# Experts two at a time on raw f32 weights, in the expert stage of a hybrid decoder layer

## The reference

```python
def hier_moe(h, ...):                       # h: (256, 1024)
    ...
    gates = jnp.sum(one_hot(e_idx, N_EXPERTS) * wts[..., None], axis=1)
    def expert(acc, prm):                   # 32 experts
        wg, wu, wd, gt = prm                # (1024,512), (1024,512), (512,1024), (256,)
        hid = jax.nn.silu(h @ wg) * (h @ wu)
        return acc + gt[:, None] * (hid @ wd), None
```

## Time and profile before

| | |
|---|---|
| Median of three runs | 739.86 us |
| Profiled execution: span, as its page gives it | 794.1 us |
| TensorE, VectorE, ScalarE busy | 771.8, 647.9, 524.6 us |
| Granted TensorE clock, mean | 0.851 |
| DMA | 249.20 MB, mean 314 GB/s |
| First gather, first gate matmul | 209.06, 212.16 us |
| Last matmuls of the scatter start | 783.99 us |

### The profile page before, as it was taken

One profiled execution on the slowest core, in us unless ns is written; L12 is line 12 of the kernel. 1 busy time (PEld: TensorE's weight loads), 2 busy tenths in 40 slices (PEclk: granted clock), 3 DMA queues, 4 the chain that ended last, 5 costly groups with the idle time before them and its releaser, 6 DMA issues.

```text
span 794.1 us, 13163 instructions
## 1 busy us (share of the span) xinstructions
PE 771.8 (97%) x4865; PEld 590.9 (74%) x4865; DVE 647.9 (82%) x579; ACT 524.6 (66%) x577; POOL 139.2 (18%) x190
## 2 busy tenths in 40 slices
PE   6999999999799999999999999999999999999994
PEld 6774774535688888888888888888888888888873
DVE  3631759656869999999899999999899999999895
ACT  4011333544577888787887888787887888787883
POOL 5400200130231122111111122111111122111000
PEclk9988888888788888888888888888888888888887
DMA  9998966943598999999999999999999999999901
GB/s 320 352 369 319 386 241 253 360 170 118 188 321 307 357 359 352 343 355 349 358 343 355 372 343 359 335 358 359 355 335 363 349 359 352 342 358 357 323 1 56
DMA packets 102153, 249.20 MB, mean 314 GB/s; under 512 B 5265, under 2 KB 5325, under 8 KB 100077
## 3 DMA queue, kind: packets, MB, share of 16 engines
q1 hardware_dynamic: 99648, 244.33, 84.9%
q0 software_dynamic: 1008, 3.31, 1.2%
q10 hardware_dynamic: 1470, 1.22, 0.5%
HBM read 247.78 MB, written 1.07 MB: 313 GB/s over the span
## 4 chain that ended last, share of the span: by engine, by line
PE 95%; DVE 2%; DMA 1%; ACT 1%; issue 0%; SPq 0%; DVEq 0%
PE PS L1558 48%; PE PS L1546 8%; PE PS L1507 6%; PE PS L1252 4%; PE PS L1296 4%; PE PS L1525 4%; PE PS L1516 4%; PE PS L1413 3%; PE PS L1308 2%; PE PS L1290 2%; DMA W<-in_w_ada_dram 1%; PE PS L1180 1%; PE PS L1451 1%; PE PS L1325 1%; PE PS L1205 1%; PE PS L1337 1%
## 5 line engine op out<-in xcount | busy, mean ns | idle before, releaser
L1092 DVE TENSOR_TENSOR WL<-W,WH 128x2048 fp32r<-128x2048 f32 x185 | 417.8, 2298 | 36.1 <-ACT WH L711 36.1
L711 ACT CAST WH<-W 128x2048 fp32r<-128x2048 f32 x185 | 346.4, 1907 | 0.0
L1558 PE MATMUL PS<-WH,XT 128*128 128x512 f32 x512 | 152.3, 422 | 1.4 <-DVE XT L1111 1.4
L1558 PE MATMUL PS<-WL,XT 128*128 128x512 f32 x508 | 148.5, 417 | 0.0
L1558 PEld LDWEIGHTS PS<-WL,XT 128*128 128x128 f32 x508 | 97.5, 192 | 30.0
L1558 PEld LDWEIGHTS PS<-WH,XT 128*128 128x128 f32 x512 | 96.7, 195 | 26.6 <-DVE XT L1111 1.5
L458 POOL COPY cur<-PG 128x2 f32 (+1 forms) x31 | 5.7, 184 | 410.0 <-PE PS L1536 409.6
L1558 PE MATMUL PS<-WH,HT 128*128 128x512 f32 x248 | 72.6, 417 | 0.5 <-issue 0.5
L1558 PE MATMUL PS<-WL,HT 128*128 128x512 f32 x248 | 72.5, 417 | 0.0
L1558 PEld LDWEIGHTS PS<-WH,HT 128*128 128x128 f32 x248 | 47.3, 191 | 15.2 <-issue 0.6
L1558 PEld LDWEIGHTS PS<-WL,HT 128*128 128x128 f32 x248 | 47.9, 193 | 14.4
(11 more groups left out here) (242 smaller groups left out, 922.7 us busy)
## 6 DMA issues: line engine op xcount, KB each, us to landing
W<-in_w_gate_dram SPq DMA_DIRECT2D x64, 1024.0 KB, 8.1
W<-in_w_down_dram SPq DMA_DIRECT2D x64, 1024.0 KB, 5.7
W<-in_w_up_dram SPq DMA_DIRECT2D x63, 1024.0 KB, 9.0
W<-in_w_ada_dram SPq DMA_DIRECT2D x16, 1024.0 KB, 7.8
W<-in_w_in_dram SPq DMA_DIRECT2D x12, 1024.0 KB, 7.5
W<-in_w_ada_dram SPq DMA_DIRECT2D x16, 512.0 KB, 5.3
W<-in_w_out_dram SPq DMA_DIRECT2D x4, 1024.0 KB, 7.3
toe<-line_dram POOLq DMA_DIRECT2D x1, 1536.0 KB, 10.7
```

Of the source, the lines that this page charges most:

```text
L711: nc.scalar.copy(WH[(UPE * odd + u) % SPLITS][:], source).then_inc(hi_ready, 1)
L1092: nc.vector.tensor_tensor(low, source, WH[(UPE * odd + u) % SPLITS][:].bitcast(f32), ALU.subtract).then_inc(lo_ready, 1)
L1558: last = nc.tensor.matmul(PS[:, bank, :], lhsT, w[:, q * 512:(q + 1) * 512], start=begin, stop=end)
```

## The change

The expert stage takes two experts, 2i and 2i+1, in each of 16 turns, with 128 token slots, 64 of each. Weights are no longer split: TensorE multiplies them as f32. The array is used as two halves of 64 columns: the even expert's tokens are stationary in columns 0 to 63 and give PSUM rows 0 to 63, the odd one's in the other half, and their matmuls alternate (L1541, L1556, L1571). A turn has 24 such pairs in place of 96 matmuls of split operands. One gather (48 matmuls of 128 columns), one prepare, one scatter and two turnings (with the plain identity, 128 columns) serve both experts. XT, SG and HT are plain f32; HID, WH, WL, HnL and stack2 go. ScalarE copies the first half of XT, VectorE the second.

A unit's rows are now read as `(h p k) f`: a partition gets four (w_down: two) neighbouring rows of the matrix, 8 KB in one piece. H3 is therefore read with a step of 4 columns and GU with a step of 2. The ring has 12 slots as before, a unit of the even and one of the odd expert after each other, and each waits for its own counter, even_used or odd_used. Units 8 to 11 of the first turn go to four extra buffers V, and their ring slots are filled with turn 1's.

The core of the diff:

```diff
-            WL.append(sb(f"WL{slot}", [P, UW], f32r))
+        W = [sb(f"W{slot}", [P, UW]) for slot in range(RING)]
+        V = [sb(f"V{n}", [P, UW]) for n in range(len(SPARES))]      # SPARES = (8, 9, 10, 11)
...
             if u < 4:
-                v = w.rearrange("l e (h k p) f -> h (l e) p k f", p=P, h=2)[u % 2]
+                v = w.rearrange("l e (h p k) f -> h (l e) p (k f)", p=P, h=2)[u % 2]
...
+                    if p == 0 and v in SPARES:
+                        sp.wait_ge(pt_mm, PAIRS)
+                        if v > SPARES[1]:
+                            sp.wait_ge(pv_mm, PAIRS)
+                            sp.wait_ge(gained, 2)
+                        fetch(v, v % 2, V[SPARES.index(v)], spare_in[v])
+                        continue
...
-                    nc.scalar.copy(WH[(UPE * odd + u) % SPLITS][:], source).then_inc(hi_ready, 1)
-                    nc.vector.tensor_tensor(low, source,
-                                            WH[(UPE * odd + u) % SPLITS][:].bitcast(f32), ALU.subtract).then_inc(lo_ready, 1)
-                    nc.vector.tensor_tensor(XT[:, :, 1, :], PS[:, 2, :].rearrange("p (k s) -> p k s", k=DC),
-                                            XT[:, :, 0, :].bitcast(f32), ALU.subtract).then_inc(xt_ready, 1)
+                    nc.vector.tensor_copy(XT[:, 4:8, :], PS[:, 3, :].rearrange("p (k s) -> p k s", k=4)).then_inc(xt_dve, 1)
...
                     for k in range(DC):
+                        first = k // 4 * FF + k % 4
                         for t in range(TT):
                             for part in range(3):
-                                last = nc.tensor.matmul(PS[:, 2, k * SLOTS:(k + 1) * SLOTS], H3[:, part, t, k * P:(k + 1) * P],
-                                                        OH[:, buf, t, 0:SLOTS], start=(t == 0 and part == 0),
+                                last = nc.tensor.matmul(PS[:, 2 + k // 4, k % 4 * P:(k % 4 + 1) * P], H3[:, part, t, first:first + FF - 3:4],
+                                                        OH[:, buf, t, :], start=(t == 0 and part == 0),
                                                         stop=(t == TT - 1 and part == 2))
...
+                def gate_up(n, i, odd):
+                    late = not (turn_in_pass(i, odd) or p)
+                    pe.wait_ge(xt_act, n + 1)
+                    if not late:
+                        pe.wait_ge(scatT_ready, n * 3 + 3)
+                    for u in range(4):
+                        if u == 1:
+                            pe.wait_ge(xt_dve, n + 1)
+                        if u == 3:
+                            transpose_gate(n)
...
+                        for which in (0, 1):
+                            unit_arrived(pe, i, odd, unit_of(u, which), p)
                         for q in range(4):
-                            bank, lhsT, begin, end = outs(q, high)
-                            last = nc.tensor.matmul(PS[:, bank, :], lhsT, w[:, q * 512:(q + 1) * 512],
-                                                    start=begin, stop=end)
-                    last.then_inc(split_used, 1)
+                            k = 4 * (u % 2) + q
+                            for which in (0, 1):
+                                rows = halves_of(which)
+                                last = nc.tensor.matmul(PS[rows, u // 2, :], XT[:, k, rows],
+                                                        unit_at(i, odd, unit_of(u, which), p)[:, q * FF:(q + 1) * FF],
+                                                        start=(k == 0), stop=(k == DC - 1))
+                                if q == 3:
+                                    last.then_inc(unit_used[which], 1)
```

More of the change, by code:

```diff
@@ L101, in sem @@
             return ctx.enter_context(nc.semaphore(name))
[L104 to L107, removed]
-            WL.append(sb(f"WL{slot}", [P, UW], f32r))
+        W = [sb(f"W{slot}", [P, UW]) for slot in range(RING)]
         X = sb("X", [P, TT, D])
-        with nc.sbuf_tensor("Hn", [P, TT, D], f32) as h:
-            Hn = h
-        HnL = sb("HnL", [P, UW], f32r)
+        Hn = sb("Hn", [P, TT, D])
         G2 = sb("G2", [P, D])
@@ L376, in _ @@
+                with sp.Fori(2 if p == 0 else 1, TURNS) as i:
+                    for v in range(UPT):
+                        sp.wait_ge(unit_used[v % 2], i * UPE + (first + v // 2 + 1 - UPE))
+                        fetch(v, i * 2 + v % 2, W[slot_of(BASE + v)], unit_in[slot_of(BASE + v)])
             stream(0)
@@ L1509, in gather, with turn_over_half @@
                                                         stop=(t == TT - 1 and part == 2))
-                    last.then_inc(gather_mm, 1)
+                        if k % 4 == 3:
+                            last.then_inc(gather_mm, 1)
+                def turn_over_half(up, done):
+                    for k in range(FC):
+                        first = up * FF + k // 2 * 2 * P + k % 2
+                        last = nc.tensor.matmul(PS[:, up, k * P:(k + 1) * P], GU[:, first:first + 2 * P - 1:2], ident[:],
+                                                start=True, stop=True)
+                    last.then_inc(done, 1)
@@ L1524, in transpose_up, with prepare @@
-                    for q in range(FC, 2 * FC):
-                        last = nc.tensor.matmul(PS[:, 0, q * SLOTS:(q + 1) * SLOTS], GU[:, q * P:(q + 1) * P], stack2[:],
-                                                start=True, stop=True)
-                    last.then_inc(gt_mm, 1)
-                def prepare(n, buf, bank=1):
-                    pe.wait_ge(onehot_ready, (n + 1) * (TT + 1))
+                    turn_over_half(1, gt_mm)
+                def prepare(n, buf, bank=0):
+                    if bank == 0:
+                        pe.wait_ge(silu_ready, n)
+                    pe.wait_ge(onehot_ready, (n + 1) * ONEHOTS)
@@ new lines, in down @@
+                def down(n, i, odd):
+                    pe.wait_ge(hid_ready, n + 1)
+                    for u in (4, 5):
+                        for which in (0, 1):
+                            unit_arrived(pe, i, odd, unit_of(u, which), p)
+                        for q in range(4):
+                            k = 2 * (u - 4) + q // 2
+                            for which in (0, 1):
+                                rows = halves_of(which)
+                                last = nc.tensor.matmul(PS[rows, 2 + q % 2, :], HT[:, k, rows],
+                                                        unit_at(i, odd, unit_of(u, which), p)[:, q * FF:(q + 1) * FF],
+                                                        start=(k == 0), stop=(k == FC - 1))
+                                if q == 3:
+                                    last.then_inc(unit_used[which], 1)
```

378 lines of the change are left out of this document (157 added, 221 removed).

## The result

The changed kernel takes **666.47 us** (median of 4 runs, 665.55 to 667.98) against 739.38 for the kernel before (737.73 to 739.90): a ratio of **0.902**, 95% interval 0.900 to 0.904. Forecast: 666. Its profiled execution took 666.02 us, a span of 664.3 at a clock of 0.984 (of the 2.4 GHz level). Every timed run of the kernel before whose clock is on record had 0.982 to 0.991, near the full clock that the prediction inferred; its profile with 0.85 was the exception.

The account below looks back on a forecast made before the run. The kernel was taken as TensorE-bound in its profile, VectorE-bound when timed, then transfer-bound after the change: 226.5 us, plus 415.5 for 168 units, 3 dips, 2 landing, then the tail, gave 662, with interplay 666 (range 648 to 708).

Parts of the forecast that it names:

- Transfers become the bound: Expert stage at full clock: 12.58 MB at 424 GB/s takes 29.7 us a turn, against TensorE's 27.7.
- The stage before was held by VectorE at 16.65 us: Old expert stage with TensorE at a higher clock: VectorE holds an expert at 17.85 - 1.2 = 16.65 us.
- 24 slots of 1.0 us against 24.0 before: nothing gained: Expert weight matmuls per turn at clock 0.85: 24 concurrent half-array pairs take 24.0 us, as the split matmuls did.
- The shared parts: Gather, scatter, prepare and turnings, once for two experts: 7.7 us a turn against 11.7, at the profile's clock.
- The four changes between halves and whole array: Array mode switches in each turn: 0.2 us each, 0.8 us per turn, bounds 0 and 2.
- The halves share the array: Matmuls on the two array halves run concurrently, read from attention lines L1357 and L1358: 0.87 us against 0.73.
- rival 3: Expert matmuls: 512-column f32 streams on the halves don't share; turn 48 us, 980 us in all, chance 0.05.
- rival 2: Gather's strided weight loads run at f32 pace: 3.3 us more for 48, turn 30.5 us, total 700; chance 0.12.
- release no slot: Weight ring: the four spare buffers free no slot; after refilling 8 units, SP stands until turn 1's first slot frees.
- Rival 1: Expert stage: TensorE at a clock between 0.85 and 1 paces; time 690 to 743 us, chance 0.15.
- Front, stream and tail: Whole-kernel sum: gates from 197, 168 units from 226.5 to 647 with dips and landing, then 3.5 and 11.3 to 662.
- interplay: Allowance taking 662 to 666 us: starved pairs leave TensorE gaps of 1.4 us, and the clock fell after earlier waits.

Follow-up runs that it names:

- Half the bytes: Changed kernel loading only the left half of every expert unit, TensorE reading it twice, every matmul kept: 654.09 us, ratio 0.885 to the kernel before.
- the old rows: Changed kernel with weight rows back at 2 and 4 KB and contiguous weight loads: 693.87 us, ratio 0.939 to the kernel before.
- half the subtraction: Kernel before with L1092's subtraction made for half the columns, TensorE reading that half twice: 735.97 us, ratio 0.9955.

## Why the prediction was right, point by point

- **Transfers become the bound: right.** Forecast 424 GB/s and 29.7 us a turn; measured 422 and 29.8. Half the bytes and the old rows give 654.1 and 693.9 us, where this theory had 655 and 690. The bound is a close one: TensorE's 28.05 us a turn stand 1.7 behind it.
- **The stage before was held by VectorE at 16.65 us: the number right, the step behind it wrong.** Scaled by the clock alone, as the prediction scales TensorE's turn, 17.85 us are 15.2, 1.4 behind VectorE. It is 16.54, so TensorE held the stage, with VectorE hard by. The number came out by luck. The 27 us expected of half the subtraction, and 12 more with the rows, weren't there: the limits lay together, VectorE 16.6, TensorE 16.5, transfers 15.8 (6.29 MB at 399 GB/s). The forecast of the changed kernel didn't rest on this gap, since its turn went by the transfers.
- **"24 slots of 1.0 us against 24.0 before: nothing gained", and 27.7 us for TensorE's turn at full clock: small misses.** The slots were to take 24.0 x 0.85 = 20.4 us and take 20.9 (6.92 + 10.40 + 3.59). The shared parts were to take 7.7 x 0.85 = 6.5 and take 7.1, as they don't follow the clock either. The four changes between halves and whole array were to add 0.8 and are inside those two figures: around the lone 16 records they come to 0.15 us (3.59, of which 8 x 0.43 = 3.44 is streaming). In sum 0.5 + 0.6 - 0.8 = 0.3 more, 28.05 us. Against the kernel before, 1.7 us are gained in the matmuls, as its 96 take 22.6 us at full clock (twice 505.86 to 515.21 and 516.02 to 517.97).
- **The halves share the array: right**, read from one line of the attention; the run with both experts on one half shows it for the streams of this stage. It costs 318 us more than the changed kernel, and the 984 us are close to rival 3's 980. That rival's limit for "slower than before" is off, though: by its own sum, 197 + 16 turns + 15, the kernel is no faster from a turn of 33.0 us on, not 33.3 + 3.
- **Strided loads (rival 2): there is a cost,** but 0.21 us for 48 loads where the rival had 3.3, and it is hidden in the changed kernel.
- **The spares "release no slot": right.** At most some 2 us, not 10, and the pause at 220 is the one that was named.
- **Rival 1, the lower clock: not seen** in any run of the changed kernel or its versions (0.981 to 0.991).
- **Front, stream and tail: the sum right by luck, two of its terms not.** The first gather came at 189.8 (forecast 194; 190.6 in the kernel before at this clock), the first gate at 193.7 (197). The stream is as forecast: turn 1's first slot frees at 224.7 (226.5), and the last landing is just after 646 (647). But the end doesn't follow the last landing: the down units are asked for last and used late. The last waited arrival is at 637.6, with 26.7 us of TensorE work and output behind it; the prediction had 647 + 15. The 9 us too late and the 12 too short almost cancel. So its terms give 662 and the measured span is 664.3. The 4 us of "interplay" that make 666 of 662 rest on no row: the prediction points at the clock falling in TensorE's gaps, but in 500:530 the granted clock is 1.00 with these gaps. Another 1.7 us lie between a span and its timed run (666.02), which the sum leaves out.

Where the 73 us come from, by the runs: TensorE's own time falls by 85 us (739.4 to the floor of 654.1). Waiting for transfers gives 40 of these back with the old rows (693.9) and 12 with rows of 8 KB (666.5). Per turn TensorE's part is 33.26 us before (twice 16.63) and 28.05 after, 5.2 less, 83 us in 16 turns. Of the 5.2 us only 1.7 are in the weight matmuls; 3.5 are in gather, turnings, prepare and scatter, which stand once for two experts (10.7 to 7.1 us). So the halves make the second expert free, and the shared parts are most of the gain. This split is a sum of rows; no run has one part without the other. With the splits in place little of it could be had, by an estimate: VectorE's 16.30 us an expert are 32.6 for two. Put first, on the kernel before, the rows would have cost 6.

## What to carry to other kernels

When two or three resources lie within a few per cent, taking one away shows next to nothing and a step can even cost; judge it on the kernel in which the others are gone. Don't scale an engine's time by the clock: measure a profile at the clock of the timed runs before naming the second bound. Where transfers pace, count buffers by what they release, keep all in rotation, and ask for units in the order of use: here the order alone was worth 10 us, and one more unit ahead, with a later return to that order, 2.4.

## What the runs showed of the hardware that was not expected

- TensorE started matmuls of the free column half ahead of waiting ones of the busy half: three records are passed in the row at 448.38. With such a case seen, don't let a semaphore rest on matmuls of different halves finishing in program order.
- At a granted clock of 1.00 instead of 0.85, the matmul of L1558 (fp32r, 512 columns, whole array, one record) goes from 0.251 to 0.232 us, 8% less where the clock gives 15%. 512 cycles of 0.85 x 2.4 GHz are just 0.251 us, 512 of 2.4 GHz 0.213, so at full clock 0.02 us of a matmul are something else. An f32 record follows the clock: on the whole array 0.50 us at 0.85 and 0.43 at full clock (L1374 of the changed kernel, 32 from 149.92 to 163.65), on halves 0.43 too (1024 cycles of 2.4 GHz are 0.427). What the fp32r form waits for, no run tells.
- A weight load of 128 bf16 columns with a step of 4 takes 118 ns in the gather of the kernel before, a contiguous one 98.
- A DMA share near 1.0 is no sign of a full stream: 1.01 goes with 374 GB/s in the kernel before, 1.04 with 394 (rows of 2 and 4 KB) and 1.02 with 423 (8 KB).
